# Row norms computed inside the stages that use them, with the inverse root as one power on GpSimd

## The reference

```python
def rmsnorm(x, g):
    x32 = x.astype(jnp.float32)
    y = x32 * lax.rsqrt(jnp.mean(x32 * x32, axis=-1, keepdims=True) + EPS)
    return (y * g.astype(jnp.float32)).astype(x.dtype)

def modulate(h, shift, scale):
    return h * (1 + scale) + shift
```

## Time and profile before

| | |
|---|---|
| time, median of 3 runs | 5169.68 us (5166.49 to 5171.69) |
| profiled execution, its own time | 5170.47 us |
| span of that execution | 5168.8 us |
| busy: TensorE, VectorE, ScalarE, GpSimd | 4579.9, 3059.6, 2293.4, 6.3 us |
| mean granted clock of TensorE | 0.94 of full |
| DMA | 827 MB, 160 GB/s |

### The profile page before, as it was taken

How to read it: one execution, slowest core, us unless ns; L and a number is a source line. 1 busy time by engine, 2 the same in 40 slices (tenths; PEclk the granted TensorE clock), 3 DMA queues, 4 the chain that set the end, 5 groups by cost and what they waited for, 6 DMA issues and landing times. The chain is left out here.

```text
span 5168.8 us, 72554 instructions
## 1 busy us (share of the span) xinstructions
PE 4579.9 (89%) x25788; PEld 3866.9 (75%) x25788; DVE 3059.6 (59%) x7216; ACT 2293.4 (44%) x4350; POOL 6.3 (0%) x20
## 2 busy tenths in 40 slices
PE   7768899999999999976699999959888698988788
PEld 2446688888888888763599987749787697987677
DVE  7545688555544444433598766755557665547655
ACT  7424333566633333221456864534435444444544
POOL 0000000000000000000000000000000000000000
PEclk9889899999999999987799999989999898989899
DMA  8401434555566666310377788845443453444343
GB/s 306 161 27 33 133 121 133 155 183 176 179 216 190 190 191 190 119 67 1 125 215 217 246 261 256 263 134 200 141 135 97 154 189 139 162 142 144 106 161 141
DMA packets 380091, 827.17 MB, mean 160 GB/s; under 512 B 31912, under 2 KB 189992, under 8 KB 362132
## 3 DMA queue, kind: packets, MB, share of 16 engines
q1 hardware_dynamic: 379800, 823.45, 49.1%
HBM read 713.12 MB, written 110.20 MB: 159 GB/s over the span
## 5 line engine op out<-in xcount | busy, mean ns | idle before, releaser
L170 DVE TENSOR_TENSOR w_low__6<-w_raw,w_high__6 128x512 fp32r<-128x512 f32 x544 | 362.4, 689 | 439.9 <-ACT w_high__6 L165 439.4
L158 PE MATMUL hidden<-hT_high,w_high__6 128*128 128x512 f32 x1152 | 456.4, 396 | 15.8 <-DVE w_low__6 L170 15.8
L160 PE MATMUL hidden<-hT_high,w_low__6 128*128 128x512 f32 x1152 | 450.5, 391 | 0.0
L159 PE MATMUL hidden<-hT_low,w_high__6 128*128 128x512 f32 x1152 | 448.8, 390 | 0.0
L170 DVE TENSOR_TENSOR w_low__11<-w_raw__2,w_high__11 128x512 fp32r<-128x512 f32 x544 | 362.9, 690 | 123.9 <-ACT w_high__11 L165 108.4
L165 ACT ACTIVATE w_high__6<-w_raw 128x512 fp32r<-128x512 f32 x544 | 324.8, 625 | 216.0 <-PE side L160 204.0
L165 ACT ACTIVATE w_high__11<-w_raw__2 128x512 fp32r<-128x512 f32 x544 | 322.5, 625 | 73.6 <-PE side__2 L160 34.9
L158 PE MATMUL hidden__3<-hT_high__2,w_high__11 128*128 128x256 f32 x1152 | 331.7, 288 | 11.6 <-DVE w_low__11 L170 11.6
L160 PE MATMUL hidden__3<-hT_high__2,w_low__11 128*128 128x256 f32 x1152 | 327.3, 284 | 0.0
L159 PE MATMUL hidden__3<-hT_low__2,w_high__11 128*128 128x256 f32 x1152 | 327.1, 284 | 0.0
L158 PEld LDWEIGHTS hidden<-hT_high,w_high__6 128*128 128x128 f32 x1152 | 216.9, 188 | 58.7 <-DVE w_low__6 L170 16.0
(11 more groups left out here) (1008 smaller groups left out, 12799.5 us busy)
## 6 DMA issues: line engine op xcount, KB each, us to landing
w_raw<-in_peer_u SPq DMA_DIRECT2D x128, 512.0 KB, 4.1
w_raw<-in_peer_v SPq DMA_DIRECT2D x128, 512.0 KB, 4.0
w_raw__2<-in_peer_u SPq DMA_DIRECT2D x128, 512.0 KB, 4.2
w_raw__2<-in_peer_v SPq DMA_DIRECT2D x128, 512.0 KB, 4.9
activated_dram<-activated SPq DMA_DIRECT2D x128, 256.0 KB, 4.4
routing_dram<-routing SPq DMA_DIRECT2D x32, 1024.0 KB, 6.5
routing_chunk<-routing_dram SPq DMA_DIRECT2D x16, 2048.0 KB, 11.4
activated_again<-activated_dram SPq DMA_DIRECT2D x128, 256.0 KB, 4.3
```

The source lines that it names most:

```text
L158: nc.tensor.matmul(out, lhs[0], rhs[0], start=start, stop=False, skip_group_check=True)
L159: nc.tensor.matmul(out, lhs[0], rhs[1], start=False, stop=False, skip_group_check=True)
L160: return nc.tensor.matmul(out, lhs[1], rhs[0], start=False, stop=stop, skip_group_check=True)
L170: return nc.vector.tensor_tensor(low, src, high.bitcast(F32), ALU.subtract)
```

## The change

A class `NormIn` holds the norm's work as pieces for each engine, and the consumer's stage calls them: squares on ScalarE, the mean on VectorE, the inverse root as mean to the power -0.5 by one instruction on GpSimd, the Newton step and the scaled rows on VectorE; then for each of the 8 chunks transposes on TensorE, the high part straight from PSUM on ScalarE (scale and shift in the same instruction), and the low part on VectorE. Where `hT` is needed later (both mixers, the hybrid mixer) or there is a shift, VectorE first writes the value and then subtracts; in the gated MLP one instruction does both. The first weight pieces are issued at the start of that stage and are split ahead of and between the chunks. `rms_rows` and `rows_to_cols` stay for the other norms; `norm_cols` and `split_cols` go. `project_cols` is unrolled, the high and low parts of `hT` are kept for the mixers' other projections, and the gate rows are loaded within `project_cols`, behind its first four weight blocks.

```diff
+class NormIn:
+    def __init__(self, nc, st, ident, xs, tiles, spans, high, low, banks, hT=None, rows=None, tmp=None):
+        self.nc, self.ident, self.xs, self.tiles, self.spans = nc, ident, xs, tiles, spans
+        self.high, self.low, self.banks, self.hT = high, low, banks, hT
+        self.n = len(tiles)
+        self.rows = rows or st.sbuf("normed_rows", [P, self.n, D])
+        self.moved = hT is None and any(shift is not None for _, _, shift in spans)
+        if self.moved:
+            self.tmp = tmp or st.sbuf("modulated", [P, 2, self.n * P])
+        self.ss, self.mean, self.root, self.inv = (st.sbuf(x, [P, self.n]) for x in ("ss", "mean", "root", "inv"))
+        (self.summed, self.meaned, self.rooted, self.own, self.scaled, self.turned, self.high_kept, self.split) = (
+            st.sem(x) for x in ("rows_summed", "means_ready", "roots_ready", "norm_dve_wrote", "rows_scaled",
+                                "rows_turned", "cols_high_kept", "cols_split"))
+        self.halved = st.sem("exponents_set")
+    def act_squares(self, act):
+        nc = self.nc
+        for k, t in enumerate(self.tiles):
+            nc.scalar.activation(self.rows[:, k, :], self.xs[:, t, :], ACT.Square, accum_out=self.ss[:, k:k + 1]) \
+                .then_inc(self.summed, 1)
+    def pool_root(self, pool):
+        self.nc.gpsimd.memset(self.root[:, :], -0.5).then_inc(self.halved, 1)
+        pool.wait_ge(self.halved, 1)
+        pool.wait_ge(self.meaned, 1)
+        self.nc.gpsimd.tensor_tensor(self.inv[:, :], self.mean[:, :], self.root[:, :], ALU.pow).then_inc(self.rooted, 1)
+    def dve_scale(self, dve):
+        nc = self.nc
+        chain = Chain(dve, self.own)
+        dve.wait_ge(self.summed, self.n)
+        nc.vector.tensor_scalar(self.mean[:, :], self.ss[:, :], 1.0 / D, EPS, ALU.mult, ALU.add).then_inc(self.meaned, 1)
+        dve.wait_ge(self.rooted, 1)
+        chain.then(nc.vector.tensor_tensor(self.root[:, :], self.inv[:, :], self.inv[:, :], ALU.mult))
+        chain.then(nc.vector.tensor_tensor(self.root[:, :], self.root[:, :], self.mean[:, :], ALU.mult))
+        chain.then(nc.vector.tensor_scalar(self.root[:, :], self.root[:, :], -0.5, 1.5, ALU.mult, ALU.add))
+        chain.then(nc.vector.tensor_tensor(self.inv[:, :], self.inv[:, :], self.root[:, :], ALU.mult))
+        for k, t in enumerate(self.tiles):
+            nc.vector.tensor_scalar(self.rows[:, k, :], self.xs[:, t, :], self.inv[:, k:k + 1], None, ALU.mult) \
+                .then_inc(self.scaled, 1)
+    def pe_turn(self, pe):
+        nb = len(self.banks)
+        for c in range(KC):
+            if c >= nb:
+                pe.wait_ge(self.split, c - nb + 1)
+            for k in range(self.n):
+                if c == 0:
+                    pe.wait_ge(self.scaled, k + 1)
+                last = self.nc.tensor.transpose(self.banks[c % nb][:, k * P:(k + 1) * P],
+                                                self.rows[:, k, c * P:(c + 1) * P], self.ident[:, :])
+            last.then_inc(self.turned, 1)
+    def act_high(self, act, c):
+        act.wait_ge(self.turned, c + 1)
+        for part, scale, shift in self.spans:
+            src = self.banks[c % len(self.banks)][:, part]
+            if shift is None:
+                last = self.nc.scalar.activation(self.high[:, c, part], src, ACT.Copy, scale=scale[:, c:c + 1])
+            else:
+                last = self.nc.scalar.activation(self.high[:, c, part], src, ACT.Identity, scale=scale[:, c:c + 1],
+                                                 bias=shift[:, c:c + 1])
+        last.then_inc(self.high_kept, 1)
+    def dve_value(self, dve, c):
+        nc = self.nc
+        dve.wait_ge(self.high_kept, c + 1)
+        for part, scale, shift in self.spans:
+            src = self.banks[c % len(self.banks)][:, part]
+            out = self.tmp[:, c % 2, part] if self.moved else self.hT[:, c, part]
+            if shift is None:
+                last = nc.vector.tensor_scalar(out, src, scale[:, c:c + 1], None, ALU.mult)
+            else:
+                last = nc.vector.tensor_scalar(out, src, scale[:, c:c + 1], shift[:, c:c + 1], ALU.mult, ALU.add)
+        last.then_inc(self.own, 1)
+    def dve_low(self, dve, c):
+        nc = self.nc
+        if self.moved or self.hT is not None:
+            src = self.tmp[:, c % 2, :] if self.moved else self.hT[:, c, :]
+            self.dve_value(dve, c)
+            dve.wait_ge(self.own, 5 + c)
+            nc.vector.tensor_tensor(self.low[:, c, :], src, self.high[:, c, :].bitcast(F32), ALU.subtract) \
+                .then_inc(self.split, 1)
+        else:
+            dve.wait_ge(self.high_kept, c + 1)
+            for part, scale, _ in self.spans:
+                last = nc.vector.scalar_tensor_tensor(self.low[:, c, part], self.banks[c % len(self.banks)][:, part],
+                                                      scale[:, c:c + 1], self.high[:, c, part].bitcast(F32),
+                                                      ALU.mult, ALU.subtract)
+            last.then_inc(self.split, 1)
@@ project_cols
+def project_cols(nc, w, nblocks, kc, src, n, dst, ring, parts=None, norm=None, loads=()):
...
+            for b in range(nblocks):
+                if b >= ring:
+                    sp.wait_ge(split, b - ring + 1)
+                sp.dma_start(wt[:, b % ring, :], w[b]).then_inc(loaded[b % ring], 16)
+                if b == ring - 1:
+                    for (to, frm), s in zip(loads, side_loaded):
+                        sp.dma_start(to, frm).then_inc(s, 16)
+            for s in side_loaded:
+                sp.wait_ge(s, 16)
...
+            if normed:
+                normed.pe_turn(pe)
+            for b in range(nblocks):
+                pe.wait_ge(split, b + 1)
+                if b >= ring:
+                    pe.wait_ge(kept, b - ring + 1)
+                for c in range(kc):
+                    if b == 0 and normed:
+                        pe.wait_ge(normed.split, c + 1)
+                    elif b == 0 and not parts:
+                        pe.wait_ge(src_split, c + 1)
+                    cut = slice(c * P, (c + 1) * P)
+                    last = three_products(nc, acc[b % ring][:, 0:n], (w_high[:, b % ring, cut], w_low[:, b % ring, cut]),
+                                          (s_high[:, c, :], s_low[:, c, :]), c == 0, c == kc - 1)
+                last.then_inc(product, 1)
...
+            if normed:
+                normed.act_squares(act)
+            make_high(0)
+            for c in range(kc):
+                if normed:
+                    normed.act_high(act, c)
+                elif not parts:
+                    high_part(nc, s_high[:, c, :], src[:, c, 0:n]).then_inc(src_high_ready, 1)
+            for b in range(1, ahead):
+                make_high(b)
+            for b in range(nblocks):
+                if b + ahead < nblocks:
+                    make_high(b + ahead)
+                act.wait_ge(product, b + 1)
+                nc.scalar.activation(dst[:, b * n:(b + 1) * n], acc[b % ring][:, 0:n], ACT.Copy).then_inc(kept, 1)
...
+            def make_low(b):
+                dve.wait_ge(high_ready, b + 1)
+                low_part(nc, w_low[:, b % ring, :], wt[:, b % ring, :], w_high[:, b % ring, :]).then_inc(split, 1)
+            if normed:
+                normed.dve_scale(dve)
+            make_low(0)
+            for c in range(kc):
+                if normed:
+                    normed.dve_low(dve, c)
+                elif not parts:
+                    dve.wait_ge(src_high_ready, c + 1)
+                    low_part(nc, s_low[:, c, :], src[:, c, 0:n], s_high[:, c, :]).then_inc(src_split, 1)
+            for b in range(1, nblocks):
+                make_low(b)
@@ norm_cols is removed
-def norm_cols(nc, ident, xs, tiles, hT, scales, shifts=None):
-    with ExitStack() as ctx:
-        xn = buffer(ctx, nc, "normed_rows", [P, len(tiles), D])
-        rms_rows(nc, [(xs[:, t, :], xn[:, k, :], D) for k, t in enumerate(tiles)], EPS)
-        rows_to_cols(nc, ident, [
-            (xn[:, k, c * P:(c + 1) * P], hT[:, c, k * P:(k + 1) * P], scales[k][:, c:c + 1],
-             shifts[k][:, c:c + 1] if shifts else None)
-            for k in range(len(tiles)) for c in range(KC)])
@@ split_cols is removed
-def split_cols(nc, src, high, low):
...
@@ gated_mlp
         psF = [[st.psum(f"sum{t}_{n}", [P, 512]) for n in range(2)] for t in range(TT)]
+        normed = NormIn(nc, st, *norm, h_high, h_low, [psF[t][n] for t in range(TT) for n in range(2)])
...
+                        if first and part == 0:
+                            pe.wait_ge(normed.split, k + 1)
...
+            normed.act_squares(act)
+            high_parts(range(1), 0, 0, up_loaded, 0)
+            for c in range(KC // 2):
+                normed.act_high(act, c)
+            high_parts(range(1, 2), 0, 0, up_loaded, 0)
+            for c in range(KC // 2, KC):
+                normed.act_high(act, c)
```

(76 more changed lines are left out.)

136 lines of the change are left out of this document (48 added, 88 removed).

## The result

The kernel after takes 5051.1 us, the median of 4 runs (5049.36 to 5059.53), against 5168.35 us of the kernel before beside it: a ratio of 0.9776, interval 0.9759 to 0.9793. The gain is 117.3 us, where 136.4 were forecast; the time lies in the forecast range and 17 us above the forecast.

A forecast was written before the change was run, and what follows sets the result against it. TensorE bounds most of the span, but waits at ten row norms, 272 us. Savings of 14.4 and 14.95 (mixers), 15.7 and 11.65 (experts), 57.8 (MLPs), 21.9 (hybrids) make 136.4: 5170.5 to 5034 us, range 5005 to 5080.

The forecast's parts named there:

- The fronts: Ten normalisation sites: stretch from the stage before to the first product, 272 us in all before; 136.4 us saved overall.
- late next: Chunks ahead of first products: VectorE sets the pace except at the MLP's first piece, 1.7 us a chunk with 512 columns.
- Rival B: Chunk chain bound by hand-offs and late banks, not VectorE's rate: 0.5 us more a chunk, 22 us, 5056; chance 0.10.
- A: GpSimd's power is slow software, 5 us with four tiles and 4 with two: 33 us come back, 5067; chance 0.17.
- D: Slower than before: the power costs more than 14.6 us a site; at 17 us, 5194; chance 0.03.
- Rival C: Products directly behind the transposes start at the high clock: up to 2 us more saved a site, 5014; chance 0.08.
- The root: Each site's norm: table load, root and reciprocal go, about 1.7 us; one GpSimd power comes, taken as 1.0.
- The drain behind a table load: Skill page's 1.38 us drain within a 2.66 us switch; prediction saw none; by the page, removal worth 14 us more.
- the memset stage stays between norm and projection: 1.0: Mixer 1: a separate memset stage ahead of the projection gives back 1.0 us of the saving.
- the clearing of semaphores runs under the squares: Start of each site: GpSimd clears the old stage's semaphores while the squares run.
- The table for the low rank: Mixer 0, rms of the low rank: without the norm's root it must load the root table itself, 1.0 us back.
- from there on every stage as long as before: Expected sign: behind each site's first product, stages keep their length; forecast wrong if they lengthen by what was won.

## Why the prediction was right, and what was off

**The fronts.** Forecast and measured stretches, us:

| site | forecast | measured |
|---|---|---|
| mixer 0 | 20.6 | 20.40 |
| experts, layer 0 | 18.3 | 18.57 |
| mixer 1 | 21.6 | 24.56 |
| experts, layer 1 | 11.15 | 11.09 |
| gated MLPs | 9.6 | 9.00 to 9.47 |
| hybrids | 12.45 | 12.06, 12.36 |

The mechanism was right: VectorE, not hand-offs, is late next, with 1.63 us a chunk where 1.7 was forecast. That the sum agrees so well, 135.0 forecast and 136.05 measured, is partly luck: mixer 1 is 3.0 us longer than forecast, and the four MLPs and two hybrids are together 1.9 shorter. Rival B falls with that, and A and D with the powers of 0.70 and 1.01 us. By the Trainium skill's ratio of 1.96 for a two-input elementwise instruction ("GPSIMD Engine Reference", section "Elementwise — side-by-side cycle accounting") the estimate was 0.4 us a power; the traces show 0.30 to 0.61 more, and the trace decides. Rival C, products at the high clock, holds for two of the four MLPs (0.36 us for the first product). Behind their first products the four MLP stages are 0.2 to 1.9 us shorter than before, 5.0 in all; the two with the high clock have 1.4 us each of that, so the clock alone doesn't explain it.

**The root.** I gave it 1.7 against 1.0, 0.7 a site. The 1.0 had no row under it, only the bounds 0.1 and 5; the powers measured 1.01 us with four tiles and 0.70 with two. What the edit saves is 0.37 us in mixer 0 and 4.4 over ten sites, since the load of the table runs beside the mean. The saving was put too large; cheaper powers with two tiles hid that. The drain behind a table load, by which the prediction reckoned 14 us more, is not seen: with the root on ScalarE the root starts 0.01 us behind the end of the load.

**Mixer 1.** The term "in mixer 1 the memset stage stays between norm and projection: 1.0" was mis-sized: it costs 24.56 - 20.42 = 4.1 us. The prediction wrote that the clearing of semaphores runs under the squares. That needs squares in the same stage, and here there were none.

**The table for the low rank** was taken as 1.0 and is a load of 1.28 us at 316.04 us in the trace.

**The step that failed** is the last one, "from there on every stage as long as before", the main reason why the gain is 117.3 us and not 136.4. It cost 21.9 us in layer 0's expert stage, by the placement of hT alone: put back ahead of the rings, with everything else of the change kept, the kernel takes 5023.2 us, 28 less than the kernel after and 11 less than the forecast. Of these 28, 21.8 are that phase. The other 6, and the 11 by which this kernel lies under the forecast, are of the size by which runs of one kernel differ (10 us for the kernel after) and by which layer 1's second phase differs (388.0 against 380.8 us in the profiled executions of these two), so I don't divide them. The prediction put what moved in memory at nothing, without a reason.

## What to carry over

Work out what a change removes, and then look at what it moves in memory: a tile allocated in another place changed the pitch of 3456 matmuls by 3%, with no wait and no change of the clock to show for it. A TensorE busy time that grows for the same instructions is a sign (take the transposes that the change itself spreads out off it first, here 15.1 of 35.9 us); compare durations of the same matmuls before and after, and try one pad. A pad moves everything behind it, so look at every phase, and at which tiles each one reads. A stage that does nearly nothing still pays for what its predecessor left, here 51 semaphores on GpSimd, and belongs behind a stage that can hide it.

## What the runs showed of the hardware that was not expected

- The pitch of 128x512 matmuls depends on where the moving and the stationary tile start modulo 128 bytes. With hT moving and the weights stationary it is 226.8 ns at distance 0 and 233.3 to 234.3 at 32, 64 and 96, over nine placements. With the weights moving and the weighed routing stationary it is lowest at 64: 228.9 ns in layer 0, where it is 233.3 at 32, and 229.2 in layer 1, where it is 234.3 at 96 and 232.7 at 0. Why the two phases differ is open.
- With 256 columns distance 64 was the fast one (459.9 to 470.6 us a phase, against 480 to 482 at 0 and 475 to 481 at 96).
- Where the work area of the other engines lies changed TensorE's pace too: 513 or 532 matmuls in 60 us, at granted clock 1.00, with hT and rings in place.
- A power on GpSimd takes 0.70 us for 128x2, 1.01 for 128x4 and 1.64 for 128x8.
- Clearing a semaphore on GpSimd takes about 77 ns (51 in 3.9 us, against 1.05 us behind a stage with 15).
